# Prompt attention unrolled over sixteen query tiles, with plain transposes of the probabilities and a per-branch scaling of the outputs

## The reference, cut to what matters

```python
def masked_softmax(s, mask):
    s = jnp.where(mask, s, NEG_INF)
    m = jnp.max(s, axis=-1, keepdims=True)
    e = jnp.where(mask, jnp.exp(s - m), 0.0)
    return e / jnp.maximum(jnp.sum(e, axis=-1, keepdims=True), 1e-30)
```

## Time and profile before

| | us |
|---|---|
| time before, median of 3 runs | 3282.19 (3277.84, 3283.11, 3282.19) |
| the profiled execution, its own time | 3281.28 |
| its span in the trace | 3279.6 |
| stage of prompt attention within it | 1621.0 to 2099.0 |
| mean granted clock of PE over the span | 0.937 |

### The profile page before, as it was taken

How to read it: one execution, slowest core, us unless ns; L and a number is a source line. 1 busy time by engine, 2 the same in 40 slices (tenths; PEclk the granted TensorE clock), 3 DMA queues, 4 the chain that set the end, 5 groups by cost and what they waited for, 6 DMA issues and landing times. The chain is left out here.

```text
span 3279.6 us, 48743 instructions
## 1 busy us (share of the span) xinstructions
PE 2924.5 (89%) x18374; PEld 2688.3 (82%) x18374; DVE 1448.3 (44%) x2808; ACT 905.5 (28%) x1537; POOL 311.1 (9%) x294
## 2 busy tenths in 40 slices
PE   4999989999999997885789789687799999999997
PEld 4889879999999996884667667433589999999996
DVE  4444455544444445013255456312326454444445
ACT  4665651111111102111245345233222111111112
POOL 3444410000000001000011011211000000000000
PEclk9999999999999998997579879888899999999999
DMA  4212133211111102102100000365322111111101
GB/s 158 110 56 110 62 105 105 64 38 38 40 50 42 47 0 87 33 26 77 35 1 1 2 1 1 125 183 158 112 58 62 42 53 49 38 38 51 38 13 53
DMA packets 168574, 193.84 MB, mean 59 GB/s; under 512 B 11431, under 2 KB 154536, under 8 KB 165679
## 3 DMA queue, kind: packets, MB, share of 16 engines
q1 hardware_dynamic: 161623, 141.58, 14.2%
q0 software_dynamic: 6816, 50.49, 4.2%
HBM read 178.30 MB, written 17.91 MB: 60 GB/s over the span
## 5 line engine op out<-in xcount | busy, mean ns | idle before, releaser
L407 ACT ACTIVATE f_act_gate<-f_act_gate 128x352 f32<-128x352 f32 x132 | 65.8, 498 | 1186.2 <-DVE f_act_gate L464 1186.1
L501 DVE SCALAR_TENSOR_TENSOR trunk<-f_down,trunk 128x352 f32<-128x352 f32 x528 | 275.8, 524 | 207.8 <-PE f_down L104 207.8
L102 PE MATMUL f_up<-f_h_hi,f_gu_hi 128*128 128x352 f32 x1056 | 344.6, 326 | 0.0
L102 PE MATMUL f_gate<-f_h_hi,f_gu_hi 128*128 128x352 f32 x1056 | 344.3, 326 | 0.0
L104 PE MATMUL f_up<-f_h_hi,f_gu_lo 128*128 128x352 f32 x1056 | 342.8, 325 | 0.0
L104 PE MATMUL f_gate<-f_h_hi,f_gu_lo 128*128 128x352 f32 x1056 | 342.5, 324 | 0.0
L102 PE MATMUL f_down<-f_a_hi,f_wd_hi 128*128 128x352 f32 x1056 | 340.6, 323 | 0.0
L103 PE MATMUL f_gate<-f_h_lo,f_gu_hi 128*128 128x352 f32 x1056 | 340.5, 322 | 0.0
L103 PE MATMUL f_up<-f_h_lo,f_gu_hi 128*128 128x352 f32 x1056 | 340.1, 322 | 0.0
L103 PE MATMUL f_down<-f_a_lo,f_wd_hi 128*128 128x352 f32 x1056 | 338.5, 321 | 0.0
L104 PE MATMUL f_down<-f_a_hi,f_wd_lo 128*128 128x352 f32 x1056 | 338.1, 320 | 0.0
(11 more groups left out here) (333 smaller groups left out, 5812.3 us busy)
## 6 DMA issues: line engine op xcount, KB each, us to landing
as_pages<-in_cache_kv_slc_dram SPq DMA_DIRECT2D x192, 128.0 KB, 2.3
f_gu_raw<-in_w_ffn_gate_dram SPq DMA_DIRECT2D x44, 512.0 KB, 4.5
f_gu_raw<-in_w_ffn_up_dram SPq DMA_DIRECT2D x44, 512.0 KB, 5.7
f_wd_raw<-in_w_ffn_down_dram SPq DMA_DIRECT2D x22, 1024.0 KB, 5.0
as_pages<-in_cache_kv_slc_dram POOLq DMA_DIRECT2D x64, 128.0 KB, 3.2
in_w_raw<-in_w_in_dram SPq DMA_DIRECT2D x4, 1304.0 KB, 5.9
x_saved<-trunk SPq DMA_DIRECT2D x1, 4224.0 KB, 16.2
trunk<-x_saved SPq DMA_DIRECT2D x1, 4224.0 KB
```

What stands on the lines that cost most here:

```text
L102: pe.matmul(out, w_hi, x_hi, start=first, stop=False)
L407: act.activation(act_gate[:, b, :], act_gate[:, b, :], ACT.Silu).then_inc(silu_done, 1)
L501: dve.scalar_tensor_tensor(xT[:, m, chunk(c)], down_bank[n % 4][:, 0:CH], 0.5, xT[:, m, chunk(c)], ALU.mult, ALU.add).then_inc(down_free, 1)
```

## The change

Six things change, all in `stage_attend_prompt`:

1. The loop over kv heads is gone. All engines run through TILES = 16 tiles and one closing round, and the `nop` instructions that stood at the waits of the loop are gone.
2. A value turn is four transposes with the identity instead of four fp32 products with diagonals. POOL's diagonals are gone, and so is the wait of the turn for them.
3. The factors of a tile (gate over sum, 4 heads x 3 branches) are made once, by DVE, in step r=0 of the next tile: five small operations (six for the first tile of a kv head). They are split in high and low part, transposed by PE to 24 rows ("f None", line 1952 after the change), and copied by ACT. At the head of each of the steps r = 1, 2, 3 PE spreads the rows of one branch over all partitions by four small products with a constant picking matrix `pick` (line 1960), and ACT copies the result (128x512) to `spread`.
4. Each branch has its own accumulation in one of the two out banks, in turn. When a branch is complete, DVE multiplies its bank by `spread` (`scale`, line 1840, 128x512), placed behind the low part of the next unit. POOL adds the three branches and the two halves (`gather`, five operations). The copies by ACT line 1738 and the additions by DVE line 1830 go away.
5. In each step the first turn stands between selected and window scores; before, all turns stood behind both. In steps r = 1, 2, 3 that turn is the spread, in r = 0 a value turn.
6. At the change of kv head the first three value units of tile 7 stand between the five key and query turns of tile 8, and the other eleven units of tile 7 are done beside the scores of tile 8. Only tile 15 has a closing round of 14 units alone.

The core of the diff:

```diff
-    def turns(qt, r):
-        return ([("q", qt + 1)] if r == 2 and qt + 1 < QT else []) + \
-            ([("v", qt - 1, u) for u in quarter(qt - 1, r)] if qt > 0 else [])
...
+    def lead(n):
+        own = [("k", n, b, half) for b in range(2) for half in range(2)] + [("q", n)]
+        values = quarter(n - 1, 0) if n else []
+        mixed = [x for pair in zip(own, values) for x in pair]
+        return mixed + own[len(values):]
...
+    def turns(n, r):
+        own = [("q", n + 1)] if r == 2 and n + 1 < TILES and not leads(n + 1) else []
+        if n == 0:
+            return own
+        values = [] if r == 0 and leads(n) else quarter(n - 1, r)
+        if r == 0:
+            return values + [("f", n - 1, None)]
+        return [("f", n - 1, r - 1)] + own + values
+
...
-                def diagonals(g, qt, pair):
...
-                    pool.tensor_tensor(diag[:, qt % 2, heads].rearrange("p r b n -> p (r b) n"),
-                                       K["ident"][:].unsqueeze(1).to_broadcast([P, 3 * PAIR, P]),
-                                       f.rearrange("p r b -> p (r b)").unsqueeze(2).to_broadcast([P, 3 * PAIR, P]),
-                                       ALU.mult).then_inc(diag_ready, 1)
...
+                def gather(n):
+                    g, qt = divmod(n, QT)
+                    pool.wait_ge(scaled_done, 3 * n + 2)
+                    pool.tensor_tensor(scaled[:, 0], scaled[:, 0], scaled[:, 1], ALU.add).then_inc(added, 1)
+                    pool.wait_ge(scaled_done, 3 * n + 3)
+                    pool.wait_ge(added, 4 * n + 1)
+                    pool.tensor_tensor(scaled[:, 0], scaled[:, 0], scaled[:, 2], ALU.add).then_inc(added, 1)
+                    pool.wait_ge(added, 4 * n + 2)
+                    pool.tensor_copy(upper[:], scaled[HD:2 * HD, 0]).then_inc(added, 1)
+                    pool.wait_ge(added, 4 * n + 3)
+                    for half, sem in enumerate((added, out_taken)):
+                        pool.tensor_tensor(mixT[half * HD:(half + 1) * HD, 2 * g:2 * g + 2, qt * P:(qt + 1) * P],
+                                           scaled[0:HD, 0, half::2, :], upper[:, half::2, :], ALU.add).then_inc(sem, 1)
+                        if half == 0:
+                            pool.wait_ge(added, 4 * n + 4)
+                    pool.wait_ge(out_taken, n + 1)
...
+                        _, n, b = x
+                        if n:
+                            act.wait_ge(scaled_done, 3 * (n - 1) + b + 1)
+                        act.activation(spread[:, b], bank[:].rearrange("p (r n) -> p r n", r=GROUP),
+                                       ACT.Copy).then_inc(hi_done, 1)
...
+                for n in range(TILES + 1):
+                    for r in range(GROUP):
+                        xs = turns(n, r)
+                        first = lead(n) if r == 0 and leads(n) else head(xs)
+                        rest = xs if r == 0 and leads(n) else xs[len(first):]
+                        for x in first:
+                            high(x)
+                        if n < TILES:
+                            exp_selected(n, r)
+                        for x in rest:
+                            high(x)
+                        if n < TILES:
+                            exp_window(n, r)
...
+                    elif x[0] == "v":
+                        v, rows = products[x], rows_of(x)
+                        dve.tensor_tensor(turned_lo[v % RING][0:rows, :], bank[0:rows, :],
+                                          turned_hi[v % RING][0:rows, :].bitcast(F32), ALU.subtract).then_inc(split, 1)
+                        if x in behind:
+                            scale(*behind[x])
                     else:
...
+                        dve.engine_nop().then_inc(split, 1)
+
+                def scale(n, b):
+                    dve.wait_ge(pv_done, products[("v", n, ends[n][b])] + 1)
+                    dve.wait_ge(hi_done, at[("f", n, b)] + 1)
+                    if n:
+                        dve.wait_ge(out_taken, n)
+                    dve.tensor_tensor(scaled[:, b], out_bank[(3 * n + b) % 2][:].rearrange("p (r n) -> p r n", r=GROUP),
+                                      spread[:, b], ALU.mult).then_inc(scaled_done, 1)
...
+                def factors(n):
...
+                    dve.tensor_scalar(factor[:], sums[:, n % 2], 1e-30, None, ALU.max).then_inc(factor_step, 1)
...
+                    dve.reciprocal(factor[:], factor[:]).then_inc(factor_step, 1)
...
+                    dve.tensor_tensor(factor[:], factor[:], z[:, qt, off:off + ROWS].rearrange("p (r b) -> p r b", b=3),
+                                      ALU.mult).then_inc(factor_step, 1)
+                    dve.wait_ge(factor_step, done + 3)
+                    dve.tensor_copy(factor_split[:, 0], factor[:]).then_inc(factor_step, 1)
+                    dve.wait_ge(factor_step, done + 4)
+                    dve.tensor_tensor(factor_split[:, 1], factor[:], factor_split[:, 0].bitcast(F32),
+                                      ALU.subtract).then_inc(factor_ready, 1)
...
+                for n in range(TILES + 1):
                     for r in range(GROUP):
-                        half = slice((r % 2) * HD, (r % 2 + 1) * HD)
-                        cols = slice(r * P, (r + 1) * P)
...
+                        else:
+                            if n < TILES:
+                                max_selected(n, r)
+                            for x in first:
+                                low(x)
+                        if n < TILES:
+                            max_window(n, r)
+                        if n and r == 0:
+                            factors(n - 1)
+                        for x in rest:
+                            low(x)
...
                         for h in range(GROUP):
-                            tr = pe.matmul(bank[0:rows, h * P:(h + 1) * P], probs[qt % 2][:, h, lo:lo + rows],
-                                           diag[:, qt % 2, h, branch, :], start=True, stop=True)
+                            tr = pe.transpose(bank[0:rows, h * P:(h + 1) * P], probs[n % 2][:, h, lo:lo + rows],
+                                              K["ident"][:])
...
+                    elif x[2] is None:
+                        pe.wait_ge(factor_ready, x[1] + 1)
+                        tr = pe.transpose(bank[0:2 * ROWS, 0:P],
+                                          factor_split[:].rearrange("p s r b -> p (s r b)").bitcast(F32), K["ident"][:])
...
+                        _, n, b = x
+                        pe.wait_ge(hi_done, at[("f", n, None)] + 1)
+                        if n == 0 and b == 0:
+                            pe.wait_ge(pick_ready, 1)
+                        for h in range(GROUP):
+                            tr = pe.matmul(bank[:, h * P:(h + 1) * P], pick[:, 3 * h + BRANCHES[b], :], factor_rows[:],
+                                           start=True, stop=True)
...
+                    b = BRANCHES.index(branch)
+                    first, last = u == (ends[n][b - 1] + 1 if b else 0), u == ends[n][b]
+                    bank = out_bank[(3 * n + b) % 2]
...
+                    if first and 3 * n + b >= 2:
+                        pe.wait_ge(scaled_done, 3 * n + b - 1)
...
+                    pe.matmul(bank[:], values, turned_hi[v % RING][0:rows, :], start=first, stop=False)
+                    pe.matmul(bank[:], values, turned_lo[v % RING][0:rows, :], start=False,
                               stop=last).then_inc(pv_done, 1)
-                    if last:
-                        pe.wait_ge(pv_done, PRODUCTS * g + v + 1 + RING)
-                        pe.nop().then_inc(out_done, 1)
...
+                def through(x):
+                    turn(x)
+                    value_product()
+                    if x[0] == "v":
+                        pending.append(x)
...
+                        if n < TILES and not (r == 0 and leads(n)):
+                            selected_scores(n, r)
+                        for x in first:
+                            through(x)
+                        if r == 0 and leads(n):
+                            selected_scores(n, r)
+                        if n < TILES:
+                            window_scores(n, r)
+                        for x in rest:
+                            through(x)
+                value_product()
```

More of the change, by code:

```diff
@@ new lines, in head @@
+    def head(xs):
+        return xs[:1] if xs and xs[0][-1] is not None else []
+    order = [x for n in range(TILES + 1) for r in range(GROUP)
+             for x in (lead(n) if r == 0 and leads(n) else []) + turns(n, r)]
+    at = {x: i for i, x in enumerate(order)}
+    dups = {x: i for i, x in enumerate([x for x in order if x[0] in "kq"])}
+    dup_order = list(dups)
+    values_order = [x for x in order if x[0] == "v"]
+    products = {x: i for i, x in enumerate(values_order)}
+    ends = [[max(u for u, unit in enumerate(value_units(n)) if unit[0] == branch) for branch in BRANCHES]
```

(13 more changed lines are left out.)

430 lines of the change are left out of this document (200 added, 230 removed).

## The result

The changed kernel takes 3297.32 us (median of 6 runs, 3296.74 to 3298.9) against 3282.59 (6 runs, 3277.84 to 3285.51): a ratio of 1.0046 with a 95% interval of 1.0033 to 1.0058. It is slower, by about 15 us. The forecast was 3263 us with a range of 3240 to 3296. The case that came nearest is the rival on the other side, the expensive tile start, which had 0.20 and 3292 us.

The account below looks back on a forecast made before the run. PE was taken to set the pace, with DVE the next limit. Terms -9 + 2 - 18 - 4 + 7 + 5 - 1 = -18 us took 3281.3 to 3263 us; likeliest case 3252 to 3273, whole range 3240 to 3296.

Parts of the forecast that it names:

- the expensive tile start: Rival, chance 0.20: at 14 tile starts, waits and clock falls cost 2.9 us instead of 0.9 each, giving 3292 us.
- the term of the tile's start: Step 0 of tiles: PE pause and lost clock +7 us, POOL and DVE blocking each other +5 us.
- the change of kv head: From tile 7's last own product to tile 9's first score: 58.2 us becomes 40, -18 us, bounds -22 and -12.
- the terms for them (-9 + 2 - 4 + 7 + 5): Full steps -9, small tiles +2, closing round -4, pause and clock at tile starts +7, POOL against DVE +5 us.
- The sign that was to tell of it: Wrong on the high side if the clock row of step 0 shows 0.5 at most of the tile starts.
- The small tiles: Tiles 0 to 3 and 9 to 11: a spread between the score groups lengthens their chains, +2 us.
- The hold-up: POOL's gather stretches DVE's factor operations with two SBUF inputs: 0.35 us on average for 14 tiles, +5 us (0 to 14).
- the walk: Step-by-step estimate of a full step after the change: DVE sets 6.6 us against 6.91, -9 us over 32 steps.
- The closing round: Last round after tile 15: units no longer wait for factors, 31.9 us becomes 28, -4 us.
- the transposes: Rival, chance 0.04: transposes leave PE at the lower clock, full steps take about 10 us, about 3350 us in all.
- The relief of PE: Rival, chance 0.15: PE's savings count fully, full steps take 5.3 to 5.7 us instead of 6.6, about 3236 us.
- The new waits: Rival, chance 0.11: waits around scalings, out banks, gather and spread eat the whole gain, 3275 to 3288 us.

Follow-up runs that it names:

- factors early and gather late: Changed kernel, with DVE making factors before the next tile's first selected maximum and POOL's gather waiting for the split factors: 3230.78 us, 0.9855 of the kernel before.
- the pause filled: Changed kernel plus nine additional PE products, results overwritten, ahead of the factor transpose in the first step of tiles 3 to 7 per kv head: 3271.53 us.
- the unrolling's: Kernel before plus only the unrolled loop and joined kv heads; turns stay products with diagonals: 3250.87 us, 28 us below the kernel before.
- the late gather alone: Changed kernel, with POOL starting the gather in a tile's first step only after DVE has split the factors: 3254.97 us, 0.992 of the kernel before.

## Why the prediction was wrong

**The step that failed** is the term of the tile's start, which the prediction put at +7 us for pause and clock and +5 us for POOL and DVE holding each other up. The mechanism was named, the pause of "some 2.7 us" came out at 2.45, but its price was taken at 0.9 us for 8 tile starts. Against the kernel before, the stretches other than the change of kv head lost 37 us, where the terms for them (-9 + 2 - 4 + 7 + 5) come to +1; the head of the stage gained 3.2 us and was put at 1. The runs put a number on what the two kept back: with factors and gather out of the way the kernel is 67 us faster. The sign that was to tell of it was wrong in place too: the clock row of step 0 was to show 0.5, and step 0 of the full tiles shows 0.89 to 1.00 (tiles 4 to 7 and 12 to 15); the clock fell in the step behind it, to 0.50 to 0.55 in tiles 4, 5, 12 and 13.

Three sizes in it were wrong.

- *What a fall of the clock costs.* I priced the stretch at the lower clock, and charged it at the full tiles. The step after the pause runs at it as a whole, 9.72 us for tile 5's r=1 against 6.2 with the pause filled, and the step behind it often starts in it. Filling the pause, with the chain as it is, brought 26 us.
- *Where it falls.* The small tiles, 0 to 3 and 9 to 11, were given +2 us and lost 19; tile 3 went from 23.7 to 31.2 us. With factors early and gather late tile 3 takes 20.1 us, at a clock of 1.00, and with the pause filled alone 22.6, so the spread between its scores costs nothing that shows; the pause and the clock did it.
- *The hold-up.* I gave it 0.35 us for a tile, on the operations with two SBUF inputs. It was 1.0 us in the example above and in most tiles (a chain of 2.07 us with the gather beside it, 1.04 without; the 1.0 us given to the five operations themselves was right), and line 1870 was held too. So the term belonged at the top of its bounds, 14 us, even before the clock. POOL's additions took 1.27 us and not the 0.98 that the diagonals' rate of the earlier trace rows had given, so a gather is 4.9 us of POOL's time and not 4, and 5.2 to 5.9 with its waits in most tiles, and meets more of DVE's.

**What was right.** The pause and its place, the 1.0 us of the factor operations, and some sizes. A turn of 128 rows at the upper clock loads in 0.43 us (median). The scaling takes 0.68 us, as the low part does. The change of kv head was put at -18 us from tile 7's last own product to tile 9's first score, 58.2 to 40 us; it took 37.0, and 20.6 us were gained over the two tiles.

**What was right only by its number.** Tile 14, at the upper clock before and after, went from 30.0 to 29.5 us, with steps of 8.5, 6.3, 7.9 and 6.7; the walk's last step was 6.6. But the walk had DVE hardly ever idle behind the first score, and in that step (which has no scaling) DVE is busy for 3.95 of 6.74 us:

```profile
2036.69:2043.43 6.74, 5.76 (x37) 4.52 (x36) 3.95 (x6) 3.95 (x10) 0.00 (x0) 1.00 0.00 0
```

DVE waits 1.24 us there for the window scores, and PE 0.98 us for a low part. What sets the step is the chain through both, not DVE's sum of work, so that 6.7 came near 6.6 was luck. Of the 9 us for 32 such steps, 0.28 each, tile 14 shows 0.5 for its four.

**What had the wrong sign.** The closing round should have gained 4 us and lost 5 with tile 15. Between the ends that the prediction took (28 us forecast, 31.9 before) it lasts 35.1 us, from 2076.3 to 2111.4: from 2082 to 2106 us, behind a pause of 2.1 us at its start, the mean clock was 0.58.

**Of the rivals**, the transposes do not hold the clock down: in the changed kernel full steps with transposes run at 1.00 (tile 14), and with products instead it came back by 0.015 for 8 us more. The rule from the Trainium skill ("TensorE: Matmul & The Clock Gate", Part 4: PE-mode transpose), that the fast clock does not engage for transposes, is not borne out here either, though these steps mix transposes with products and only the earlier trace rows have transposes alone. The relief of PE (3236 us) is in part real: once the pause is gone, cheap turns are worth 32 us. That the kernel then comes to 3231 us is chance, since 28 us of the gain are the unrolling's, and the full steps are not the rival's of 5.3 to 5.7 us: one step each of tiles 4 and 12 takes 5.2, those of tiles 5 and 6 take 6.2 to 7.9. The new waits did not eat the gain: neither PE nor ACT waits for a scaling or a gather in the trace, and the scalings themselves wait 1.8 us in all. The expensive start was to decide from "over 2.6 us more than now". By the prediction's own base, which gained 30, the 15 us that the kernel lost make 45 us for 14 starts, 3.2 each.

The Trainium skill ("SBUF — State Buffer", Who interferes with whom) says that the loser waits for the whole instruction of the other, and that a DVE operation with at most one SBUF input isn't concerned unless it is in a two-port mode. The trace agrees: the product with two SBUF inputs was stretched to as much as 1.07 us beside an addition of 1.27, and operations with one input in PSUM were not held: in the changed kernel 28 of the 148 low parts and 4 of the 48 scalings overlap an operation of a gather, and all of these take 0.670 to 0.692 us. Reciprocals and casts of the factors, with one SBUF input, overlap one 13 times each and kept their 0.23 and 0.17 us. Line 1870, a scalar operation with one SBUF input, was held (least 0.161, median 0.586, most 0.877 us); the page names that kind among those that can enter such a mode, and casts too, which here were not held.

## What to carry to other kernels

Ask of each pause what the engine's clock does in the step behind it; here a pause of 2.45 us cost 3.5 us more in the step after it, and moving five tiny operations and one wait was worth 67 us. Before work is moved to POOL, look at which DVE operations with SBUF operands stand on a path that PE waits for, and start POOL's work behind them. A gain on the engine that seems to be the bound (the cheap turn) can be 8 us with the stall and 32 without it, so a part that "brings nothing" is to be tried again when the next stall is gone.

## What the runs showed of the hardware

A DVE operation on 128x12 elements with two inputs in SBUF, 0.17 us by itself, takes up to 1.07 us when a POOL addition on SBUF runs; reciprocals and casts of the same size did not suffer. Additional products whose results nobody reads made a kernel faster by 26 us, since the granted clock stayed at 1.00 through the step behind them, as in tiles 3 to 5 and 11 to 13. One kernel can keep the clock at a tile in one execution and, it seems, lose it in the next: the late gather alone gave 3253 to 3256 us four times and 3270 once, and only of the last is there a trace.
